# Fused decoder layer: sixteen sums per feed-forward group on VectorE instead of GpSimd, w_down rows asked for earlier, 24 of 60 shares of the cache copies issued in the input projection

## The reference: what is computed

```
z = rmsnorm(x) @ w_in                        # 1024 x 3584, feeds retention and attention
mix = concat(retention(z), dilated_attention(z, cache_k, cache_v)) @ w_out
x = x + rmsnorm(mix)
gate, up = split(rmsnorm(x) @ w_gu)          # 1024 x (2 x 2816)
x = x + rmsnorm((silu(gate) * up) @ w_down)  # 2816 x 1024
k_new, v_new = concat(cache, new)[:, T:]     # caches of the samples, moved on by 8 rows
```

## Time and profile before

| What | Value |
|---|---|
| median of the runs | 1895.47 us (1894.05, 1895.47, 1910.42) |
| the profiled execution | 1913.38 us |
| its span, first to last instruction | 1911.4 us |
| TensorE busy | 1548.1 us, 81% |
| VectorE, ScalarE, GpSimd busy | 826.7, 554.6, 596.8 us |
| DMA | 317.76 MB, 166 GB/s on the mean |
| mean granted TensorE clock | 0.914 of full speed |

### The profile page before, as it was taken

One profiled execution on the slowest core, in us unless ns is written; L12 is line 12 of the kernel. 1 busy time (PEld: TensorE's weight loads), 2 busy tenths in 40 slices (PEclk: granted clock), 3 DMA queues, 4 the chain that ended last, 5 costly groups with the idle time before them and its releaser, 6 DMA issues.

```text
span 1911.4 us, 23143 instructions
## 1 busy us (share of the span) xinstructions
PE 1548.1 (81%) x8974; PEld 1320.5 (69%) x8974; DVE 826.7 (43%) x1212; ACT 554.6 (29%) x1046; POOL 596.8 (31%) x534
## 2 busy tenths in 40 slices
PE   8999999988888989989696679568767992865667
PEld 6788888875556767889696668568767871654445
DVE  3232111167655434568454346335534650422235
ACT  4300222113544443333132123122322340332232
POOL 3354100143222102564464256236524530000000
PEclk9999999989999999999898899789888996887778
DMA  5333341467313983426865686677568599998644
GB/s 186 125 116 117 119 159 47 161 191 218 100 56 132 418 318 111 127 78 206 199 170 135 152 188 149 139 185 175 131 146 210 170 271 148 223 220 183 175 142 154
DMA packets 138253, 317.76 MB, mean 166 GB/s; under 512 B 23884, under 2 KB 65116, under 8 KB 132997
## 3 DMA queue, kind: packets, MB, share of 16 engines
q1 hardware_dynamic: 129352, 229.26, 36.4%
q0 software_dynamic: 6976, 71.32, 21.1%
q10 hardware_dynamic: 1824, 15.83, 2.0%
HBM read 254.45 MB, written 137.92 MB: 205 GB/s over the span
## 4 chain that ended last, share of the span: by engine, by line
DMA 24%; POOL 12%; PE 9%; DVE 7%; issue 4%; ACT 2%; SPq 1%; another core or an unknown queue 1%; POOLq 0%; ACTq 0%; DVEq 0%
DMA raw_d<-w_down 14%; DMA raw_step<-wt_scratch 7%; PE y_ps L2658 6%; DVE slot_lo L2460 4%; DMA raw_step<-w_down 3%; ACT slot_hi L2289 1%; PE y_ps L2739 1%; POOL xm L1696 1%; POOL h_lo L1708 1%; SPq L2101 1%; POOL t L2192 1%; POOL t_down L2221 1%; POOL t L2199 1%; POOL f_sum L2209 1%
## 5 line engine op out<-in xcount | busy, mean ns | idle before, releaser
L2658 PE MATMUL y_ps<-h_hi,slot_hi 128*128 128x320 f32 (+1 forms) x560 | 190.1, 339 | 150.4 <-DVE f L2471 150.4
L2658 PEld LDWEIGHTS y_ps<-h_hi,slot_hi 128*128 128x128 f32 x560 | 112.4, 201 | 153.2 <-DVE slot_lo L2460 149.8
L504 PE MATMUL z_ps<-w_hi,h_hi 128*128 128x512 f32 x488 | 191.3, 392 | 4.3 <-POOL h_lo L332 4.3
L504 PE MATMUL z_ps<-w_lo,h_hi 128*128 128x512 f32 x488 | 190.6, 391 | 0.0
L2460 DVE TENSOR_TENSOR slot_lo<-raw_step,slot_hi 128x512 fp32r<-128x512 f32 x132 | 88.4, 712 | 234.6 <-ACT slot_hi L2289 234.4
L2658 PE MATMUL y_ps<-h_lo,slot_hi 128*128 128x320 f32 (+1 forms) x560 | 188.1, 336 | 0.0
L2658 PE MATMUL y_ps<-h_hi,slot_lo 128*128 128x320 f32 (+1 forms) x560 | 187.7, 335 | 0.0
L504 PE MATMUL z_ps<-w_hi,h_lo 128*128 128x512 f32 x432 | 168.6, 390 | 0.0
L2460 DVE TENSOR_TENSOR slot_lo<-raw,slot_hi 128x512 fp32r<-128x512 f32 x104 | 142.2, 1385 | 41.3 <-ACT slot_hi L2289 41.3
L2289 ACT CAST slot_hi<-raw_step 128x512 fp32r<-128x512 f32 x132 | 75.2, 618 | 248.7 <-DMA raw_step<-wt_scratch 145.9
L2190 POOL TENSOR_TENSOR t<-raw 128x512 f32<-128x512 f32 x20 | 29.9, 1496 | 335.7 <-DVE slot_lo L2460 324.7
(11 more groups left out here) (359 smaller groups left out, 3467.4 us busy)
## 6 DMA issues: line engine op xcount, KB each, us to landing
ks_sample<-cache_k_win POOLq DMA_DIRECT2D x60, 544.0 KB, 13.0
vs_sample<-cache_v_win POOLq DMA_DIRECT2D x60, 544.0 KB, 15.7
raw<-w_gu SPq DMA_DIRECT2D x20, 1024.0 KB, 16.6
raw_step<-f_scratch SPq DMA_DIRECT2D x66, 256.0 KB, 4.3
K<-cache_k_win SPq DMA_DIRECT2D x8, 2048.0 KB
w_raw<-w_in SPq DMA_DIRECT2D x14, 1024.0 KB
z_scratch<-z_out SPq DMA_DIRECT2D x56, 256.0 KB, 2.0
raw_d<-w_down SPq DMA_DIRECT2D x11, 1024.0 KB, 28.4
```

The source lines that it names most:

```text
L504: mm = pe.matmul(z_ps[t % 3][:, :], x[:, k, t * 128:t * 128 + 128], w[:, par, k, :], start=(k, n) == first, stop=(k, n) == last)
L2658: mm = pe.matmul(bank[:, 0:cols], w, v[:, k, :], start=fresh and (k, m) == (0, 0), stop=(k, m) == (HK - 1, 2), skip_group_check=True)
```

## The change

Three edits.

1. `third`, `fourth`, `sums_of_f` and `differences_of_down` move from GpSimd to VectorE, word for word but for one more wait in the first `sums_of_f`. They are put between VectorE's other operations of the chains: `third(g, 1)` and `fourth(g, 1)` at i = 2 and 3 of the first half of a group, `sums_of_f(g - 1)` at i = 4, `third(g + 1, 0)` and `fourth(g + 1, 0)` at i = 2 and 3 of the second half, and `differences_of_down(g)` at i = 6, behind the first split of `raw_d` of the same group (before: `differences_of_down(g - 1)` late in the first half of group g).
2. On SP, `load_down(g)` stands straight behind `load_gate_up(g + 1, 0)`, and `store_t(g)` at the group's end.
3. Of the 60 shares 24 are issued in the input projection, one at every second tile from the tenth on; 32 in the chains, one or two for each half, released by TensorE's second product of the half; four in the second half of the feed-forward (steps 5, 16, 27 and 38).

Of the four moved functions the diff shows `third` as removed and as added, and the head of `sums_of_f`; the others are moved in the same way.

```diff
+SHARE, COPIED_FIRST = (L - DEC_T) // 60, 24
...
+                def copies(k, t):
+
+                    n = at(k, t) - TT
+                    if n % 2 and n < 2 * COPIED_FIRST:
+                        copy_windows(pool, A, kept, n // 2 * SHARE, SHARE)
+
                 for k in (*ROTATED, GATED):
                     for t in range(TT):
                         finish(k, t)
+                        copies(k, t)
+                for k in range(GATED + 1, GROUPS):
+                    for t in range(TT):
+                        pool.wait_ge(z_evac, at(k, t) + 1)
+                        copies(k, t)
...
+    PACED = [(24 + 8 * n // 5, 24 + 8 * (n + 1) // 5) for n in range(Count.CHAINS)]
...
                 out.all_stored(sp)
+                store_t(0)
                 for g in range(1, GROUPS):
                     store_f(g - 1)
                     if g < LAST:
@@ -2142,20 +2157,19 @@
                     else:
                         load_step(0)
                         load_step(1)
+                    load_down(g)
                     store_f_sums(g - 1)
-                    store_t(g - 1)
-                    load_down(g)
                     if g < LAST:
                         load_gate_up(g + 1, 1)
                     else:
                         load_step(2)
                         load_step(3)
+                    store_t(g)
...
                 store_f_sums(LAST)
                 load_step(6)
-                store_t(LAST)
                 load_step(7)
...
-                def third(g, hh):
-                    c = Count.chain(g, hh)
-                    pool.wait_ge(raw_landed[hh], 16 * g + 16)
-                    if c:
-                        pool.wait_ge(lo_ready, gate_up(*((g, 0) if hh else (g - 1, 1)), 4) + 1)
-                    pool.tensor_tensor(t3[:, :, :], part_of(hh, 1, 1), part_of(hh, 0, 1), ALU.subtract).then_inc(t_ready, 1)
-                    pool.wait_ge(t_ready, 4 * c + 1)
-                    pool.tensor_tensor(t2[:, :, :], t3[:, :, :], part_of(hh, 0, 0), ALU.add).then_inc(t_ready, 1)
...
+                    c = Count.chain(g, hh)
+                    dve.wait_ge(raw_landed[hh], 16 * g + 16)
+                    if c:
+                        dve.wait_ge(lo_ready, gate_up(*((g, 0) if hh else (g - 1, 1)), 4) + 1)
+                    dve.tensor_tensor(t3[:, :, :], part_of(hh, 1, 1), part_of(hh, 0, 1), ALU.subtract).then_inc(t_ready, 1)
+                    dve.wait_ge(t_ready, 4 * c + 1)
+                    dve.tensor_tensor(t2[:, :, :], t3[:, :, :], part_of(hh, 0, 0), ALU.add).then_inc(t_ready, 1)
...
+                def sums_of_f(g):
+                    dve.wait_ge(f_ready, 6 * g + 6)
+                    if g:
+                        dve.wait_ge(f_sum_stored, 64 * g)
+                    else:
+                        dve.wait_ge(s_ready, 3)
+                        dve.wait_ge(s3_formed, 3)
...
-                third(1, 0)
...
-                fourth(1, 0)
                 for g in range(1, GROUPS):
-                    copies(4 * g - 4, 4 * g - 2)
-                    third(g, 1)
-                    sums_of_f(g - 1)
-                    fourth(g, 1)
-                    copies(4 * g - 2, 4 * g)
-                    differences_of_down(g - 1)
-                    if g < LAST:
-                        third(g + 1, 0)
-                        fourth(g + 1, 0)
-                sums_of_f(LAST)
-                differences_of_down(LAST)
+                    for hh in range(2):
+                        pool.wait_ge(done, made(g, hh, 1))
+                        copies(*PACED[2 * g - 2 + hh])
                 pool.wait_ge(half_set, 2)
                 root(0)
-                for p in range(5):
-                    pool.wait_ge(done, stepped(GROUPS * p))
-                    copies(40 + 4 * p, 42 + 4 * p)
+                for p in range(4):
                     pool.wait_ge(done, stepped(GROUPS * p + 5))
-                    copies(42 + 4 * p, 44 + 4 * p)
+                    copies(56 + p, 57 + p)
...
                 unit(3)
+                third(1, 0)
                 for n in range(8, 12):
                     low(n)
+                fourth(1, 0)
                 low_of_sum(1, 0)
                 unit(4)
                 low_of_sum(2, 3)
+                differences_of_down(0)
...
                         low_ahead(gate_up(g, 0, i) + LEAD)
                         if i == 1:
                             add_gate(g, 0, 2, 0, 0)
+                        if i == 2:
+                            third(g, 1)
                         if i == 3:
                             for m in range(4):
                                 low_ahead(down(g - 1, m) + LEAD)
+                            fourth(g, 1)
+                        if i == 4:
+                            sums_of_f(g - 1)
                         if i == 5:
                             add_gate(g, 1, 7, 1, 1)
...
@@ -2585,6 +2596,12 @@
                             add_up(g, 0, 2, 0, 0, 0)
                             dve.wait_ge(done, made(g, 1, 3))
                             times(g, 1, rest_ps[0], 0, 2)
+                        if i == 2 and g < LAST:
+                            third(g + 1, 0)
+                        if i == 3 and g < LAST:
+                            fourth(g + 1, 0)
+                        if i == 6:
+                            differences_of_down(g)
                         if i == 5:
                             sample_low_part(g, 0)
                             add_up(g, 1, 7, 2, 1, 1)
...
                     sample_low_part(g, 1)
+                sums_of_f(LAST)
                 for s in range(STEPS):
```

58 lines of the change are left out of this document (26 added, 32 removed).

## The result

The changed kernel takes 1634.39 us in the median of 4 runs (1633.31 to 1639.63), beside 1897.28 us of the kernel before (1894.05 to 1910.42): ratio 0.8609, 95% interval 0.8564 to 0.8654. Its profiled execution took 1639.63 us, with a span of 1637.8 us at a mean granted clock of 0.972 (before 0.914).

The account below looks back on a forecast made before the run. TensorE was taken to stall on late raw_d loads held up by cache copies, which also slowed the steps. Terms -167 + 1 - 115 + 5 = -276 from the profiled 1913.4 gave 1637, taken as 1630 us; range 1595 to 1650, 57%.

Parts of the forecast that it names:

- w_down sooner, chains: Chains, groups 1 to 10: earlier request makes raw_d land in time, the stall goes, 46.7 us a group; -167 us.
- Sums on VectorE: Chains: 16 moved operations a group run beside TensorE's work; some cost ahead of group 1; +1 us (-3 to +5).
- Rival 1: Chains: VectorE becomes the binding engine at 58 us a group, 1740 us, or halfway, 1683; chance 6% together.
- Rival 5: Input projection, blocks 1 and 2: GpSimd's issues, slowed by VectorE, bind the tiles; +6 us, 1636 us; chance 2%.
- Copies, second half: Feed-forward's second half: 16 of 20 shares leave; steps 0 to 45 gain 92 us, the last stretch 23; -115 us.
- The loop of raw_last: Step 45 to the last product: SP's requests for raw_last stay 10.9 us a pair of steps; TensorE needs 5.5.
- Copies, input projection: Input projection: 24 shares delay z stores behind weights and zr, a short stall in block 5; +5 us (0 to +40).
- The rest: Behind the last product: nothing changes, 0 us.
- Rivals 2 and 3: Chains: transfers collide and step gaps stay, 1700 us, 24%; or raw_d, requested sooner, still lands late, 1752 us, 5%.
- rival 2: Chains: w_gu's second half or stores collide with new bursts, 5 us a group; step gaps stay; 1700 us; chance 24%.
- Rival 4: Input projection: copies hold z stores and weights, stopping TensorE; slower overall from some 11 us a share; chance 4%.

Follow-up runs that it names:

- e5: Changed kernel with the request for w_down put back behind the stores of f's sums in SyncE's queue; 1633.38 us.
- e12: Changed kernel with the old order around w_down: its differences formed in the next group, then stored, then the new rows requested; sums stay on VectorE; 1639.11 us.
- e4: Changed kernel with the sums of weights and of f left on GpSimd; 1639.16 us.
- e3: Kernel before with only the cache copies moved to their new places; sums on GpSimd and late w_down request stay; 1727.79 us.
- e8: Changed kernel with the last product's operands loaded and split beside steps 20 to 62, one pair every four steps; 1593.98 us.
- e10: Changed kernel with no cache copies in the input projection's block 5; five shares beside block 6, 33 in the chains; 1626.17 us.
- e2: Changed kernel with the cache copies put back where they were before; 1729.78 us.
- e1: Kernel before with only the new order: w_down requested sooner, its differences formed in the same group's second half, by GpSimd; old copies; 1738.95 us.

## Why the prediction was right, and where it was not

The time was forecast at 1630 us, 4 us from the measured one. Its sum, -276 us, was measured as -273.6 us of span. The terms are less exact than the sum, and that it came so near is in part luck: the chains gained 13 us more than forecast and the rest 4, the second half gained 8 less and the projection cost 10 more.

**w_down sooner, chains: -167, measured -180.** 585.6 - (1314.9 - 906.0) = 176.7, and 3.0 in group 10. The times within a group were right: request +14 for +15, landing at some +23 for +27, ScalarE's asking at +38 for +40. Mis-sized is the 46.7 us a group. TensorE's own time is 45.3, not 46, and the 0.7 us for small waits is not there with the sums on VectorE (with GpSimd it is: 46.4). The end of the range at -174, "none for small waits", was thus too near.

**Its cause was put in the wrong step.** The prediction gave the gain to the request's place in SyncE's queue. e5 undoes a part of that place at no cost. e12 undoes the whole new order and e4 the move to VectorE, for some 5 us each in the medians and 11 to 13 us in the profiles' chains, where the stall had cost 180. The request was late for the differences that had to be formed first, 34 us into a group; that edits 1 and 2 each remove this was not seen. The prediction did read that raw_d was "asked for between two bursts of two shares", but not that one share fewer ahead of it would be enough, as e3's groups show.

**Sums on VectorE: +1, measured +1.6** (from the projection's end to group 1, 530.2 against 528.6). The splits fell to 0.69 us as forecast, so far that 17 more instructions cost VectorE nothing. Rival 1 is dead: 29.8 us of 45.3. Rival 5 did not come: no issue took over 786 ns, the median is 553. The figure of the Trainium skill, page "SBUF — State Buffer", section "A bandwidth-pool intuition that's wrong (but worth ruling out)", is for a DMA beside a VectorE copy. Here VectorE's instructions are TENSOR_TENSOR, all 53 of a group, and SCALAR_TENSOR_TENSOR or TENSOR_TENSOR in the projection from 88 to 340 us; so these traces, the one before too, speak against the rival and do not test the figure. (Of the 60 issues before, 40 stand in the chains, not 32 as the prediction says.)

**Copies, second half: -115, measured -107.** Steps 0 to 45 took 137.7 us for 130, the last stretch 99.7 for 98 to 100. The 8 us are the stall ahead of step 1, which the 4 us "for small gaps at the start" were meant to hold; the bound of 15 us of gaps held them. The loop of raw_last, at 10.3 us a pair for 10.9, was read rightly, and e8 shows its cause.

**Copies, input projection: +5, measured +15.5.** Place and cause were right, block 5 behind weights and zr, and e10 shows it. The size was not: 11.4 us for 5, with matmuls 0.43 us apart behind it, where they had been 0.23, and 1 us at two other tiles. The first tile of block 5 was in its buffer at 274.5 us, its store was asked for at 280.94 and landed at 316.0. The step had 34 us against 21.7, less some 7 for a pause in copying. It was 41.5 from tile to landing, a pause in copying from 291 to 318 us included and 6 of them in SyncE's queue, held by zr, against the 31 us until TensorE stopped at 305.4. ScalarE's 13.55 us of waiting for the weights ended at 303.36; they lie beside the store's wait and add nothing to it.

**The rest: 0, measured -3.6.** All kernels with the old copies beside the steps have 43.7 to 43.9 us there, all others 38.9 to 40.2. The mechanism wasn't tried; the granted clock of that stretch rose from 0.89 to 0.93.

Rivals 2 and 3 did not come; the margin was larger than feared, as e2 shows at a DMA share of 0.95. It hangs on where the bursts stand, though: e1, at their old places, has rival 2's collision in two groups. Rival 4 came at 0.65 us a share (15.5 / 24), far from the 11.3 at which it decides.

## What to carry to other kernels

When a load is late, ask what has to read its buffer before it may be overwritten, and on whose queue that reader stands; here a queue of slow small operations made it late, and a burst of two shares just ahead of it made the lateness cost something; several edits would have cured it. Take bulk copies to stages whose DMA engines are idle, but keep them out of the few stretches that ask for large loads ahead of latency-bound stores. When a stage runs at a fixed time per turn with no engine and no DMA full (10.3 us, 61 of 88 us, 0.46), look for a request queued behind a wait that depends on the request just ahead of it; asking for these loads sooner and spreading them gave 40 us, more than all the copies still cost.
